# First modulation of a two-block fp32 transformer computed by halves of the channels, on one Trainium2 core

## The reference, cut to what matters

```python
sc, scc = silu(c), silu(c_ctx)
mod_x = sc @ w_mod[0] + b_mod[0]
mod_c = scc @ w_mod[0] + b_mod[0]
shift, scale, gate = split(mod, 3)
hx = rms_norm(x, g_pre) * (1 + scale_x) + shift_x
hc = rms_norm(ctx, g_pre) * (1 + scale_c) + shift_c
q_lat, kv_lat, q, k, v, ... = split(h @ w_in)
```

## Time and profile before

| | us |
|---|---|
| median of 3 runs | 3040.29 (3038.69 to 3043.32) |
| the profiled execution, its own time | 3050.49 |
| span of its trace, first to last instruction | 3048.7 |
| PE busy in the span | 2974.1 (98%) |
| first matmul of `three_units` starts at | 49.38 |
| first matmul of `qa` 0 starts at | 76.29 |

### The profile page before, as it was taken

The page is one execution under the profiler, slowest core; times in us unless marked ns, Lnnn a source line. Parts: engine busy times, 40 slices in busy tenths (PEclk is TensorE's granted clock), DMA queues, the critical chain, the costliest instruction groups (busy, mean ns, idle before and its releaser), DMA issues.

```text
span 3048.7 us, 44661 instructions
## 1 busy us (share of the span) xinstructions
PE 2974.1 (98%) x17911; PEld 2439.6 (80%) x17911; DVE 1552.4 (51%) x2051; ACT 1197.6 (39%) x2017; POOL 1098.7 (36%) x561
## 2 busy tenths in 40 slices
PE   8999999999999999999999999999999999999999
PEld 6877688888888877788888877788878877788887
DVE  4364546563223586622323876477753876454420
ACT  3255431212223455423234445544332545544422
POOL 1302032423344222055456321345554321345543
PEclk9999999999999999999999999999999999999999
DMA  7102024342222233344434212146665312123332
GB/s 231 37 8 42 1 71 138 90 132 69 64 63 67 58 96 91 91 116 106 112 96 120 62 45 62 36 133 185 187 186 167 85 46 62 48 84 97 97 97 90
DMA packets 442377, 279.73 MB, mean 92 GB/s; under 512 B 113610, under 2 KB 419516, under 8 KB 441788
## 3 DMA queue, kind: packets, MB, share of 16 engines
q1 hardware_dynamic: 442172, 276.87, 32.6%
HBM read 274.73 MB, written 2.10 MB: 91 GB/s over the span
## 4 chain that ended last, share of the span: by engine, by line
PE 55%; DVE 3%; POOL 2%; ACT 1%; issue 1%; DMA 1%; ACTq 0%; DVEq 0%; SPq 0%; POOLq 0%
PE ps L732 33%; PE ps L1543 4%; PE ps L1052 2%; PE ps L1604 2%; PE ps L1611 2%; PE ps L1633 2%; PE ps L991 1%; PE ps L1323 1%; POOL WL L2627 1%; PE ps L1678 1%; PE ps L902 1%; PE ps L1353 1%; PE ps L1334 1%; PE ps L1709 1%; PE ps L1578 1%
## 5 line engine op out<-in xcount | busy, mean ns | idle before, releaser
L2627 POOL TENSOR_TENSOR WL<-RAW,WH 128x1024 fp32r<-128x1024 f32 (+2 forms) x335 | 804.7, 2402 | 1516.7 <-ACT WH L1929 1490.8
L732 PE MATMUL ps<-HH,WH 128*128 128x512 f32 (+1 forms) x2080 | 690.0, 369 | 6.0 <-POOL WL L2627 4.9
L732 PE MATMUL ps<-HH,WL 128*128 128x512 f32 (+1 forms) x2080 | 686.0, 367 | 0.0
L732 PE MATMUL ps<-HL,WH 128*128 128x512 f32 (+1 forms) x2080 | 682.7, 366 | 0.0
L1929 ACT ACTIVATE WH<-RAW 128x1024 fp32r<-128x1024 f32 (+2 forms) x335 | 346.4, 1034 | 408.2 <-PE ps L732 255.8
L732 PEld LDWEIGHTS ps<-HH,WH 128*128 128x128 f32 x2080 | 358.7, 188 | 81.1 <-POOL WL L2627 12.2
L732 PEld LDWEIGHTS ps<-HH,WL 128*128 128x128 f32 x2080 | 357.1, 188 | 64.9
L732 PEld LDWEIGHTS ps<-HL,WH 128*128 128x128 f32 x2080 | 356.8, 188 | 65.0
L2967 DVE SCALAR_TENSOR_TENSOR XT<-RAW,CS,XT 128x1024 f32<-128x1024 f32 x77 | 134.7, 1750 | 37.0 <-DMA RAW<-in_w_ada 36.1
L732 PE MATMUL ps<-FH,WH 128*128 128x512 f32 x308 | 120.6, 392 | 0.9 <-POOL WL L2627 0.8
L732 PE MATMUL ps<-FH,WL 128*128 128x512 f32 x308 | 120.0, 390 | 0.0
(11 more groups left out here) (557 smaller groups left out, 5722.6 us busy)
## 6 DMA issues: line engine op xcount, KB each, us to landing
RAW<-in_w_in SPq DMA_DIRECT2D x122, 512.0 KB, 3.9
RAW<-in_w_ada SPq DMA_DIRECT2D x96, 512.0 KB, 3.9
RAW<-in_w_up SPq DMA_DIRECT2D x88, 512.0 KB, 4.3
RAW<-in_w_in SPq DMA_DIRECT2D x72, 256.0 KB, 3.7
RAW<-in_w_mod SPq DMA_DIRECT2D x32, 512.0 KB, 3.7
RAW<-in_w_down SPq DMA_DIRECT2D x32, 512.0 KB, 4.7
WMOD<-in_w_mod SPq DMA_DIRECT2D x8, 1024.0 KB, 14.2
RAW<-in_w_branch SPq DMA_DIRECT2D x16, 512.0 KB, 3.4
```

The lines of the kernel that those rows point to most:

```text
L732: ins = nc.tensor.matmul(ps[0:width, t0:t0 + tn], a, b[:, k0 + k, tokens0 + t0:tokens0 + t0 + tn], start=first and k == 0 and i == 0, stop ...
L2627: nc.gpsimd.tensor_tensor(wl[:, 0:used], RAW[n % NRAW][:, 0:used], wh[:, 0:used].bitcast(F32), ALU.subtract).then_inc(*up(w_low))
```

## The change

- `w_mod` comes in two halves of the channels. The 4 loads of the columns for channel tiles 0 to 3 (shift and scale) come first, then the three weight units, then the 4 loads for tiles 4 to 7.
- `first_modulation(p)` makes one 128x1024 result of a half; it is copied once, turned by 8 plain transposes, and DVE sums the four groups with one reduction. `PICK` is gone.
- The second half is done inside `three_units`: its products before channel tile 2, its transposes before tile 3. DVE takes it up between tiles 3 and 4 of `apply_norm` (`midway`).
- In layer 0 the three units go side by side, tile by tile (`lags = (0, 0, 0)`); the third unit has the spare place `X2` with no wait, and ACT splits it before tile 1. The squares of `qlb` lie in other places (`SQQ`).
- Four matmuls without use stand before the units' first tile in place of six.
- Token statistics: ACT squares the untransposed blocks with a row sum, takes the root of 6 columns; DVE takes the reciprocal of 128x6; PE spreads it by 6 transposes; ACT copies it to `RSTD`. DVE, in place of ACT, copies the turned blocks to `XT`.

```diff
-                lags = (0, LAG, 2 * LAG) if l else (0, 1, KD)
+                third = ("E0", (0, "oc", 5)) if l else ("X2", None)
+                lags = (0, LAG, 2 * LAG) if l else (0, 0, 0)
                 for i in range(KD + lags[2]):
+                    if between:
+                        between(i)
                     for n in range(3):
...
+                        if l == 0 and k == 0 and n == 0:
+                            for _ in range(4):
+                                nc.tensor.matmul(groups[0][:, 0:512], ones, WMOD[:, 0, 0:512], start=True, stop=True)
                         if n == 0:
                             pe.wait_ge(norm_low, at(norm_low, (l, "h", k)))
...
+            def first_modulation(p):
+                ps = open_group(("mod1", 0, "rows", p), 3)
+                for c in range(FIRST_CHUNKS):
+                    for first in range(2):
+                        pe.wait_ge(mod_in[4 * c + 2 * p + first], 16)
+                        for k in range(4 * first, 4 * first + 4):
+                            g = 32 * (k % 4)
+                            ins = nc.tensor.matmul(ps[g:g + 32, 512 * c:512 * c + 512], CWIDE[:, k, :],
+                                                   WMOD[:, c * KD + k, 512 * p:512 * p + 512],
+                                                   start=first == 0, stop=first == 1, tile_position=(0, g))
+                ins.then_inc(*up(product_ready, ("mod1", 0, "rows", p)))
+            def first_columns(p):
+                got(("mod1", 0, "rows", p))
+                ps = open_group(("mod1", 0, "columns", p), 3)
+                for j in range(2 * 4):
+                    ins = nc.tensor.transpose(ps[:, j * P:(j + 1) * P], MROWS[:, j * P:(j + 1) * P], ident)
+                ins.then_inc(*up(product_ready, ("mod1", 0, "columns", p)))
...
-                three_units(l, T)
+                three_units(l, T, None if l else lambda i: first_modulation(1) if i == 2 else first_columns(1) if i == 3 else None)
...
+            modulation_loads(0)
             for n, (key, loads, split, _, _) in enumerate(units):
...
                 if n == NRAW - 1:
+                    modulation_loads(1)
                     for b in range(1, len(VECTOR_BATCHES)):
...
             for tb in range(NTB):
-                A(XT[:, :, tb * P:(tb + 1) * P], ps[:, :].rearrange("p (k t) -> p k t", t=P), ACT.Copy).then_inc(
-                    *freed(("xT", tb)))
+                A(SQX[:, :], XIN[:, tb, :], ACT.Square, accum_out=RSUM[:, tb:tb + 1]).then_inc(
+                    *up(act_out, ((0, "pre"), "sq", tb)))
+            A(RCOL[:, 0:NTB], RSUM[:, 0:NTB], ACT.Sqrt, bias=epsb[:, 0:1], scale=1.0 / DM).then_inc(
+                *up(act_out, ((0, "pre"), "root")))
...
                     for k in range(KD):
+                        if k == 1:
+                            ahead((l, "qlb", 2), 0)
                         high_shifted((l, "h", k), HH[:, k, :], NT, lambda s: MOD1[l][:, k, s:s + 1])
...
                 for k in range(KD):
+                    if midway and k == KD // 2:
+                        low(k - 1)
+                        midway()
                     gv = value_of[k] = value(keys[k])
...
+            def first_modulation(p):
+                key = ("mod1", 0, "rows", p)
+                ps = ready(key)
+                V.tensor_copy(MROWS[:, :], ps[:, :]).then_inc(*freed(key))
+                key = ("mod1", 0, "columns", p)
+                ps = ready(key)
+                V.tensor_reduce(MSUMS[:, :, :, :].rearrange("p c j v -> p (c j) v"),
+                                ps[:, :].rearrange("p (a g r) -> p a r g", g=4, r=32)[:, :, 0:2, :], AX.X,
+                                ALU.add).then_inc(*freed(key))
...
+                for v in range(2):
+                    step(V.tensor_tensor(into[:, :, :, v:v + 1], MSUMS[:, :, :, v:v + 1], bias, ALU.add))
+                pre_gains(0, 4 * p, 4 * p + 4)
...
-                    apply_norm([(l, "h", k) for k in range(KD)], XT, scale, shift, RSTD, HH, HL, NT)
+                    apply_norm([(l, "h", k) for k in range(KD)], XT, scale, shift, RSTD, HH, HL, NT,
+                               midway=lambda: first_modulation(1))
```

More of the change, by code:

```diff
@@ L1088, in turn_vectors @@
                 ins.then_inc(*up(product_ready, ("vec", b0)))
[L1090 to L1100, removed]
@@ L1125, in _ @@
             pe.wait_ge(act_out, at(act_out, "silu_c"))
             first_modulation(0)
[L1127 to L1134, removed]
@@ L1135, in _ @@
-            held[0] = None
-            for _ in range(6):
-                nc.tensor.matmul(columns[:, 512:1024], ones, WMOD[:, 0, 0:512], start=True, stop=True)
+            first_columns(0)
             def z_load(l, b, j):
@@ L1838, in _, with modulation_loads @@
             vector_loads(0, vec0_in)
[L1839 to L1843, removed]
+            def modulation_loads(p):
+                for c in range(FIRST_CHUNKS):
+                    for first in range(2):
+                        t0, k0 = 512 * p, 4 * first
+                        src = D["w_mod"][k0 * P:(k0 + 4) * P, c * CHUNK + t0:c * CHUNK + t0 + 512]
+                        sp.dma_start(WMOD[:, c * KD + k0:c * KD + k0 + 4, t0:t0 + 512],
+                                     src.rearrange("(k p) n -> p k n", p=P)).then_inc(mod_in[4 * c + 2 * p + first], 16)
+            modulation_loads(0)
             for n, (key, loads, split, _, _) in enumerate(units):
@@ L1997, in _ @@
             A(CS[:, 16:24], VEC[:, COLUMN["c2", 0]:COLUMN["c2", 0] + 8], ACT.Silu).then_inc(*up(act_step, "cs"))
-            root((0, "pre"), NT, DM, RSTD)
+            ps = ready((0, "pre"))
+            A(RSTD[:, 0:NT], ps[:, 0:NT], ACT.Copy).then_inc(*freed((0, "pre")))
             act.wait_ge(dve_step, at(dve_step, "lb_max"))
@@ L2908, in apply_norm @@
                         dve.wait_ge(split_value, led.count[split_value.name])
-                    if k:
+                    if k and not (midway and k == KD // 2):
                         low(k - 1)
@@ L2926, in _ @@
             for tb in range(NTB):
[L2927 to L2930, removed]
+                ps = ready(("xT", tb))
+                V.tensor_copy(XT[:, :, tb * P:(tb + 1) * P], ps[:, :].rearrange("p (k t) -> p k t", t=P)).then_inc(
+                    *freed(("xT", tb)))
             keep_vectors(0, 1)
-            inverse_root((0, "pre"), RSTD, NT)
+            dve.wait_ge(act_out, at(act_out, ((0, "pre"), "root")))
+            V.reciprocal(RCOL[:, 0:NTB], RCOL[:, 0:NTB]).then_inc(*up(to_pe, ((0, "pre"), "rows")))
             raw = VEC[:, COLUMN["b_lb", 0]:COLUMN["b_lb", 0] + 8].rearrange("p (d l t) -> p d l t", d=2, l=2)
```

83 lines of the change are left out of this document (31 added, 52 removed).

## The result

| 19 runs each, beside one another | median, us |
|---|---|
| kernel before | 3044.49 (3038.69 to 3049.59) |
| changed kernel | 3050.02 (3042.92 to 3055.64) |

The account below looks back on a forecast made before the run. PE, busy 98% of the span, was taken as the bound, its start bound by the 8 MB of `w_mod`. 6.6 us won at `qa` 0 less 1.7 for the clock gives 4.9: 3040.3 to 3035.4 us, 8 in 10 within 3031.5 to 3040.

Parts of the forecast that it names:

- Loads, statistics, columns: Start: fourth load lands at 24.8 us, statistics hidden by loads, copy to 27.9, transposes to 30.0; second half about 41.6.
- third rival: Second half of modulation late or dear: loads 4 us after 41.6 or transposes at 0.27; 3036.6 to 3039.5 us; chance 0.20.
- First product at 35.2: Three units' first product at 35.2 us, bounds 33.6 to 37.0, 14.2 us before 49.38.
- bias and gains 0.82: DVE's bias and gains after the reduction, before the first tile: 0.82 us, to 31.1.
- Units end 66.8, `qa` 0 at 69.7: Three units end at 66.8 us; `qa` 0 starts at 69.7 in place of 76.29, 6.6 us won.
- The waits themselves: New PE waits: 1.4 us before tile 4 for DVE, 2.1 us before `qa` 0 for its split.
- The clock behind that wait costs 1.7: After the 2.1 us wait before `qa` 0 the clock falls to 1.2 GHz, costing 1.7 us (bounds 0 and 1.7).
- After `qa` 0 every load waits for a split, so the rest moves along: From `qa` 0 to the end: the rest of the kernel keeps the start's lead, 4.9 us less.
- The first one: Rival: no fall of the clock behind the new wait before `qa` 0; 6.6 us won, 3033.7 us; chance 0.20.
- My slower rival: Three units at the low clock, kernel about 3055 us; with 13 us of work at half speed, 3043.5; chance 0.05.
- a change under 6.1 us can't be told from none: Whole kernel's time: a change under 0.2% (6.1 us) is indistinguishable from none; forecast 0.16%, just inside.

Follow-up runs that it names:

- POOL quiet: Changed kernel without POOL's subtractions for units 1 and 2, ACT writing plain copies (part of the computation left out); one execution, `qa` 0 starts at 69.66 us.
- second comparison: Changed kernel unaltered, again beside the kernel before (3047.3 us, 27 runs) on one chip: 3050.43 us, ratio 1.0011 (1.0002 to 1.0020).

## Why the prediction was wrong, point by point

- *Loads, statistics, columns*: right. The fourth load's products began at 24.48 (24.8 forecast), lasted 1.94 (1.8), the copy ended at 27.8 (27.9), the transposes at 29.9 (30.0). The second half waited for no load, and cost 3.64 and 1.03; the rows' 0.13 for a transpose held, and the third rival's 0.27 did not come.
- *First product at 35.2*: it was 36.32. The term "bias and gains 0.82" was mis-sized: POOL's subtraction held up the additions, and it was 2.5 from 30.18 to the first `GV` at 32.71. With POOL quiet it was 34.67, 0.57 of this from the earlier load.
- *Units end 66.8, `qa` 0 at 69.7*: 69.48 and 72.49. Besides 1.1 from the first product, the `GV` pair that POOL held up added a wait of 0.82 before tile 1 and so put off the second half, which came at 44.06 instead of 41.6. With POOL quiet: 66.65 and 69.66. That this meets the forecast to 0.1 is in part luck: counted from the fourth load's products the forecast had 44.9 to `qa` 0, the quiet run 45.75, the changed kernel 48.01. So POOL is about 2.3 of the 3.1 missing there, and the rest stays open. I had priced DVE's and POOL's work each from rows in which the other was idle; rows 6 and 7 held the overlap's ingredients, not the overlap. The waits themselves were right: 1.58 before tile 4 (1.4), 2.19 before `qa` 0 (2.1).
- *The clock behind that wait costs 1.7*: in some executions. The window 72 to 74 us has the clock at 1.00 in the first profile of the changed kernel and at 0.50 in the second:

```profile
72.00:74.00 2.00, 1.51 (x8) 1.33 (x9) 0.00 (x0) 1.75 (x3) 2.00 (x2) 1.00 0.15 33
```

```profile
72.00:74.00 2.00, 2.00 (x7) 1.68 (x7) 0.00 (x0) 0.60 (x1) 1.65 (x1) 0.50 0.76 171
```

- *"After `qa` 0 every load waits for a split, so the rest moves along"*: this is the step that failed. The rest did move along, all engines by 3.77 us, until a fixed PSUM slot met one that the change had shifted: the rotation of query tile 3, in slot 2 in place of 3. Cost: 2.26 of wait and the clock behind it, 3.7 together, which was the whole lead in the profile; 4.3 between medians side by side. The order of the instructions does not show it; the slot numbers do, and I never counted them.
- *The rivals*: none was this one. The first one's condition, no fall of the clock behind the new wait, held in one of the two profiles. My slower rival was the three units at the low clock, which did not come: in the changed kernel's profile the clock was up from 34 us to the wait at 151. Its sums were wrong besides: 13 us of work at half speed cost 13, which makes 3048.4 and not 3043.5, and all of the 30.2, less the waits and the clock's fall that they replace, makes some 3060 and not 3055.
- *Two smaller readings*: by rows 3 the clock fell at 32.45, not 32.3 (0.95 over the half microsecond up to 32.5), which changes nothing. And that a change under 6.1 us can't be told from none did not hold: 19 runs each told 4.9 us from nothing.
- *The sum mended*: -4.9 + 2.8 (late `qa` 0) + 3.7 (slot) = 1.6 slower, and 1.7 less in an execution where the clock holds behind `qa` 0. Measured were 4.9 (2.7 to 6.7) and 3.4 (0.6 to 6.1). Much of the difference is clock. The mean granted clock of each execution is on record, and in the second comparison it was 0.9931 for the changed kernel, 0.9944 for the kernel before and 0.9943 with tile 3 in slot 3. With the two levels that gives, as an estimate, 8.2 us more at 1.2 GHz for the changed kernel than for the one before, which costs at most 4.1 us. Then -3.8 (`qa` 0) + 2.3 (wait) + 4.1 (clock) is 2.6 slower, inside the second interval and just below the first. Two falls, behind `qa` 0 and behind the slot, make 3.4 us of these 4.1; that they came in most of the executions is not shown, since only two were profiled. With tile 3 in slot 3, `qa` 0 starts at 72.99, 3.3 ahead, and the runs show 3.0 and 1.2 won.

## What to carry to other kernels

When a change takes groups out of a rotating pool of buffers, or gives them fixed places, list who gets which place before and after, to the end of the program, and look where a fixed place follows on a rotating one: a wait can appear far from the edit. Price two engines' operations from rows where they run beside each other, VectorE's with two SBUF inputs beside GpSimd's above all. And follow a lead along the whole stream: the offset between two aligned traces shows in one line where it goes. Take more than one profile before a lead is priced: the same kernel started `qa` 0 at 68.99 and at 70.50.

## What the hardware showed unexpectedly

The same stream of products runs at one of two paces, with PE busy throughout and the clock at 1.00. The window of 200 us in the kernel before and in the run with all slots moved by one:

```profile
700.00:900.00 200.00, 200.00 (x1134) 173.38 (x1133) 57.10 (x64) 42.03 (x45) 72.48 (x32) 1.00 0.24 64
```

```profile
700.00:900.00 200.00, 200.00 (x1156) 174.90 (x1155) 59.15 (x66) 44.52 (x48) 73.89 (x33) 1.00 0.24 64
```

That is 1.9% more products in the same time, 3.9 us over this stretch: a pair of products of 512 and 256 columns takes 353.3 ns or 346.7, and from 720 to 900 us every profile kept one of the two. Three of the fourteen had the faster one: all slots moved by one, the kernel before with tile 3 in slot 2, and the one with POOL quiet. The changed kernel had x1134 in both its profiles. Which pace a stretch falls into was not tried by itself, and neither was what sets it. Together with the clock's falls, which come behind the same wait in one profile and not in another, it is of the size of the differences measured here, and one profile of each kernel could not have told them apart: the profiles of before and after lay 2.2 us apart where the medians lay 5.5.
